# Experts' weights as the stationary operand in 24 up groups of a dense expert layer

## The reference, cut to what matters

```
q = h @ w_q; s1, s2 = scores of q's halves against two sets of 128 keys
e = ids of the 16 best pairs of each head;  w = softmax of their scores
act = gelu(u[e] . h) * w          # u: 16384 x 2048
y   = sum over heads and picks of act * vt[e]
x   = x + ga2 * y;  out = rmsnorm(x) * g_final
```

## Time and profile before

| | us |
|---|---|
| median of 3 runs | 3324.61 |
| lowest, highest | 3324.33, 3324.92 |
| the profiled execution | 3331.73 |
| its span, first to last instruction | 3330.1 |

### The profile page before, as it was taken

One profiled execution on the slowest core, in us unless ns is written; L12 is line 12 of the kernel. 1 busy time (PEld: TensorE's weight loads), 2 busy tenths in 40 slices (PEclk: granted clock), 3 DMA queues, 4 the chain that ended last, 5 costly groups with the idle time before them and its releaser, 6 DMA issues.

```text
span 3330.1 us, 41040 instructions
## 1 busy us (share of the span) xinstructions
PE 3311.5 (99%) x15198; PEld 2742.1 (82%) x15198; DVE 2232.1 (67%) x2112; ACT 1542.3 (46%) x1184; POOL 730.4 (22%) x559
## 2 busy tenths in 40 slices
PE   9999999999999999999999999999999999999999
PEld 8888888888787888878888888888888888888887
DVE  6674545688888788866677497444444777777777
ACT  7343334443333333353465346777776333333333
POOL 0000003400000000121000188888882000000000
PEclk9999999999999999999999999999999999999999
DMA  7555556888888888867555466777777666666663
GB/s 285 186 192 195 190 191 242 306 308 336 307 309 305 297 306 319 310 249 296 212 190 211 169 215 215 214 222 215 217 221 259 230 234 229 230 236 228 229 226 128
DMA packets 159557, 803.92 MB, mean 241 GB/s; under 512 B 51668, under 2 KB 52484, under 8 KB 70496
## 3 DMA queue, kind: packets, MB, share of 16 engines
q1 hardware_dynamic: 85728, 610.05, 50.3%
q0 software_dynamic: 67248, 170.03, 16.2%
q10 hardware_dynamic: 6480, 22.44, 1.8%
HBM read 759.23 MB, written 43.18 MB: 241 GB/s over the span
## 4 chain that ended last, share of the span: by engine, by line
PE 92%; DVE 3%; DMA 2%; issue 1%; ACT 1%; POOL 0%; SPq 0%; DVEq 0%; POOLq 0%; ACTq 0%
PE ps L2149 28%; PE ps L2151 28%; PE ps L2150 28%; PE ps L2189 2%; DVE adaacc L1532 2%; DMA adaraw<-in_w_ada 1%; PE ps L2226 1%; PE ps L2228 1%; PE ps L2227 1%; DMA raw<-in_w_first 1%; ACT hi L641 1%; PE ps L2337 0%; PE ps L2317 0%; DVE modrow L1543 0%; PE ps L2676 0%
## 5 line engine op out<-in xcount | busy, mean ns | idle before, releaser
L641 ACT CAST hi<-raw 128x2048 fp32r<-128x2048 f32 x571 | 1091.2, 1912 | 1617.9 <-PE ps L2151 1600.7
L1225 DVE TENSOR_TENSOR lo<-raw,hi 128x2048 fp32r<-128x2048 f32 x436 | 997.7, 2291 | 379.3 <-ACT hi L641 364.3
L2149 PE MATMUL ps<-hi,hT 128*128 128x512 f32 x2928 | 1152.4, 394 | 0.0
L2151 PE MATMUL ps<-hi,hT 128*128 128x512 f32 x2928 | 1140.4, 389 | 0.0
L2150 PE MATMUL ps<-lo,hT 128*128 128x512 f32 x2928 | 1139.9, 389 | 0.0
L2149 PEld LDWEIGHTS ps<-hi,hT 128*128 128x128 f32 x2928 | 549.9, 188 | 116.0 <-issue 4.8
L2151 PEld LDWEIGHTS ps<-hi,hT 128*128 128x128 f32 x2928 | 549.7, 188 | 115.6
L2150 PEld LDWEIGHTS ps<-lo,hT 128*128 128x128 f32 x2928 | 550.1, 188 | 111.0
L2011 DVE TENSOR_TENSOR lo<-raw,ps 128x2048 fp32r<-128x2048 f32 x96 | 219.7, 2288 | 297.6 <-ACT ps L1118 297.6
L581 POOL DMA_INDIRECT w_scratch<-picks,cell x256 | 396.7, 1550 | 80.1 <-issue 78.7
L2149 PE MATMUL ps<-hi,pactTh 128*128 128x512 f32 x992 | 388.7, 392 | 0.0
(11 more groups left out here) (415 smaller groups left out, 2668.9 us busy)
## 6 DMA issues: line engine op xcount, KB each, us to landing
raw<-in_w_peer SPq DMA_DIRECT2D x256, 1024.0 KB
raw<-in_w_ffn SPq DMA_DIRECT2D x132, 1024.0 KB
adaraw<-in_w_ada POOLq DMA_DIRECT2D x96, 1024.0 KB, 7.0
raw<-in_w_first SPq DMA_DIRECT2D x86, 1024.0 KB
raw<-in_w_second SPq DMA_DIRECT2D x72, 1024.0 KB
raw<-in_w_merge SPq DMA_DIRECT2D x28, 1024.0 KB
w_scratch<-zeros POOLq DMA_DIRECT2D x16, 1024.0 KB, 13.2
wc<-w_scratch POOLq DMA_DIRECT2D x32, 512.0 KB, 5.1
```

What stands on the lines that cost most here:

```text
L641: nc.scalar.copy(hi[:, s, :], raw[:, s, :]).then_inc(hi_done, 1)
L1225: V.tensor_tensor(lo[:, s, :], raw[:, s, :], hi[:, s, :].bitcast(F32), ALU.subtract).then_inc(lo_done, 1)
L2149: T.matmul(out, th[stat], hi[:, s, cut], start=start, stop=False)
L2151: return T.matmul(out, tl[stat], hi[:, s, cut], start=False, stop=stop)
```

## The change

In the up groups from number 8 (EARLY_TOP) on, 24 of 32, the operands change places. `expert_piece` takes 128 x 128 of the weights as stationary operand; the moving one is `hT[:, :, kt, :]`, both parts of the activations side by side (512 columns), for `hi`, and `hTh` alone (256 columns) for `lo`. That is 16 matmuls of 512 and 16 of 256 a piece. A tile of 128 experts stands in one bank: columns 0-255 hold hi x hTh + lo x hTh, columns 256-511 hold hi x hTl. Four tiles fill banks 0 to 3. ACT copies each second half into `gacc` (`second_halves`), DVE adds the first half (`expert_tiles`), ACT applies gelu to `gacc` in SBUF, and the store follows. Experts are on partitions now, so the product needs no turn: `peer_hi` and `peer_lo` read `pact` in SBUF.

Groups 0 to 7 keep the old up product; their hidden values are turned ahead of the product with the weights (`hidden_turn`), out of `hid`, and DVE multiplies out of PSUM. The dense weights lie in DRAM by expert (`w_d` is [16384, 256]), so the places of the picks, the clearing and the loads of `wc` change. One semaphore is merged into another on POOL.

Core of the diff:

```diff
# PE
+            def expert_piece(q, s, free):
+                pe.wait_ge(lo_done, 4 * q + (s + 1))
+                for e in range(4):
+                    if s == 0:
+                        free(e)
+                    for k in range(4):
+                        kt = 4 * s + k
+                        cut = slice(512 * k + P * e, 512 * k + P * e + P)
+                        if s == 0:
+                            T.matmul(ps[:, e, :], hi[:, s, cut], hT[:, :, kt, :], start=k == 0, stop=False)
+                            ins = T.matmul(ps[:, e, 0:SEQ], lo[:, s, cut], hTh[:, kt], start=False, stop=False)
+                        else:
+                            T.matmul(ps[:, e, 0:SEQ], lo[:, s, cut], hTh[:, kt], start=False, stop=False)
+                            ins = T.matmul(ps[:, e, :], hi[:, s, cut], hT[:, :, kt, :], start=False, stop=s == 3 and k == 3)
+                    if s == 3 and e < 3:
+                        ins.then_inc(sem("u_tile"), 1)
+                ins.then_inc(piece_used, 1)
+            def taken_out(g):
+                return lambda e: pe.wait_ge(sem("u_out"), 4 * g + (e + 1 - 4 * (EARLY_TOP + 1)))
+            expert_group(EARLY_TOP, lambda e: pe.wait_ge(sem("gelu"), EARLY_TOP - 1 + e // 2))
+            expert_group(EARLY_TOP + 1, taken_out(EARLY_TOP + 1))
+            def hidden_turn(g, u, m):
+                pe.wait_ge(sem(f"hid_in{u}"), 16 * m + 16)
+                if not isinstance(g, int) or g > 0:
+                    pe.wait_ge(sem("peer_product"), g)
+                turn(4, lambda k, m: hid[:, u, m, P * k:P * k + P]).then_inc(sem("peer_tr"), 1)
+            def first_turns(s):
+                if s == 1:
+                    pe.wait_ge(lo_done, 4 * (Q_PEER + EARLY))
+                if s in (1, 2):
+                    hidden_turn(s - 1, s - 1, 0)
+            expert_group(EARLY - 1, taken_out(EARLY - 1), first_turns)
...
-                    if j == 0:
-                        pe.wait_ge(sem("gelu"), b + 1)
                     if j < 4:
-                        wide_piece(q, s, 0)
+                        expert_piece(q, s, lambda e: pe.wait_ge(sem("y_sum"), 4 * b + 2))
# ACT
+            def second_halves(g, used):
+                for e in range(4):
+                    if e < 3:
+                        act.wait_ge(sem("u_tile"), 3 * g + (e + 1 - 3 * EARLY_TOP))
+                    else:
+                        act.wait_ge(piece_used, used)
+                    nc.scalar.copy(gaccT[:, SEQ * e:SEQ * e + SEQ], ps[:, e, SEQ:2 * SEQ]).then_inc(sem("pq_out"), 1)
             def early_group(g, u, copied=True):
                 for s in range(4):
+                    if s == 3 and not (isinstance(g, int) and g < EARLY_TOP):
+                        act.wait_ge(sem("hid_st"), 16 * g)
+                        second_halves(g, 4 * g + 4 * (Q_PEER + 1))
                     round_piece(g + (Q_PEER + 1), s)
...
-                gelu(g, u)
+                if isinstance(g, int) and g < EARLY_TOP:
+                    gelu(g, u)
+                    return
+                gelu_turned(g, 4 * g + 4 * (1 - EARLY_TOP))
+                store_turned(g)
             def peer_hi(b, u):
-                act.wait_ge(sem("peer_tr"), b + 1)
-                nc.scalar.copy(pactTh[:, u], quarters(4)).then_inc(sem("peer_hi"), 1)
+                act.wait_ge(sem("peer_product"), b + 1)
+                nc.scalar.copy(pactTh[:, u], pact[:]).then_inc(sem("peer_hi"), 1)
# DVE
+            def expert_tiles(g):
+                for e in range(4):
+                    dve.wait_ge(sem("pq_out"), 4 * g + (e + 5 - 4 * EARLY_TOP))
+                    tile = gaccT[:, SEQ * e:SEQ * e + SEQ]
+                    V.tensor_tensor(tile, ps[:, e, 0:SEQ], tile, ALU.add).then_inc(sem("u_out"), 1)
+            with dve.Fori(EARLY_TOP + 1, EARLY) as g:
+                for s in range(4):
+                    if s == 3:
+                        expert_tiles(g - 1)
+                    copied_rest(g, s)
# POOL
-                    part = w_d[16 * i:16 * i + 16].rearrange("t (a n) -> (t a) n", n=2048)
+                    part = w_d[1024 * i:1024 * i + 1024].rearrange("(r a) t -> r (a t)", a=8)
-            w_cells = w_d.rearrange("t (e o) -> (t e) o", o=1)
+            w_cells = w_d.rearrange("e (t o) -> (e t) o", o=1)
```

More of the change, by code:

```diff
@@ L144 @@
     "gy_T": "ACT: gelu of the turned gates", "qk_T": "DVE: turned queries and keys out of PSUM",
-    "wf_in": "DMA: forget weights", "wf_zero": "Pool: zeros around their two parts", "wfh": "ACT: their leading part", "wfl": "DVE: and rest; then identity and causal mask rounded", "f_mm": "PE: forget logits",
+    "wf_in": "DMA: forget weights", "wfh": "ACT: their leading part", "wfl": "DVE: and rest; then identity and causal mask rounded", "f_mm": "PE: forget logits",
     "lg_abs": "DVE: logits' size, then -|lambda|", "lg_exp": "ACT: their exponentials", "cum": "DVE: sums of log gates",
-    "sel_in": "Pool: zeros, then ones around the log gates' sums, then a row of zeros", "pair_in": "DMA: sums of four heads as rows", "scores2": "PE: heads' scores", "max2": "DVE: maxima",
+    "sel_in": "Pool: zeros around the forget weights, zeros, then ones around the log gates' sums, a row of zeros", "pair_in": "DMA: sums of four heads as rows", "scores2": "PE: heads' scores", "max2": "DVE: maxima",
     "exp2": "ACT: exponentials (two a head)", "turned2": "PE: turned probabilities", "probs2": "DVE: these out of PSUM",
@@ L158 @@
     "out2": "DVE: chunks out of PSUM", "out2_sum": "DVE: chunks added to x",
-    "pq_out": "ACT: query chunks out of PSUM", "pq_tr": "PE: turned", "pq_T": "DVE: turned chunks out of PSUM",
+    "pq_out": "ACT: query chunks, then second halves of tiles of experts, out of PSUM", "pq_tr": "PE: turned", "pq_T": "DVE: turned chunks out of PSUM",
     "keys_in": "DMA: both key sets", "key_scores": "PE: scores against them", "sc_out": "DVE: scores out of PSUM",
@@ L167 @@
     "hid_in1": "DMA: back, odd groups", "wc_in0": "DMA: weights of a group, slot 0", "wc_in1": "slot 1",
-    "peer_product": "DVE: hidden values times weights", "peer_tr": "PE: turned", "peer_hi": "ACT: leading part",
+    "u_tile": "PE: a group's first three tiles of experts", "u_out": "DVE: tiles of experts added from both halves",
+    "peer_product": "DVE: hidden values times weights", "peer_tr": "PE: first groups' hidden values turned", "peer_hi": "ACT: leading part",
     "peer_lo": "DVE: rest", "y_sum": "DVE: chunks out of PSUM, from two", "tail_in": "DMA: second gate", "gain_in": "DMA: last gains",
@@ L1147, in _ @@
                     peer_hi(0, 0)
-            gelu(EARLY - 1, 0, out=False)
+            gelu_turned(EARLY - 1, 4 * (EARLY - EARLY_TOP))
             def down_group(b, u, turn=True):
@@ L2098, in _ @@
                     dve.wait_ge(sem("peer_hi"), b + 2)
[L2099 removed]
+                    V.tensor_tensor(hTl[:, 0:4], pact[:], hTh[:, 0:4].bitcast(F32), ALU.subtract)\
                         .then_inc(sem("peer_lo"), 1)
```

150 lines of the change are left out of this document (85 added, 65 removed).

## The result

The changed kernel takes 3349.99 us in the median of 4 runs (3346.6 to 3351.48), the kernel before 3324.57 us beside it: a ratio of 1.0076, with a 95% interval of 1.0063 to 1.0088. The change costs 25.4 us; the forecast was 22.6. The profiled run took 3351.48 us with a span of 3349.9.

What follows compares the result with a forecast made beforehand. PE was taken to set the pace, at full clock. Turns -22.1, matmuls +9.7, borders +31.0, entry +2.3 and group 31 +1.7 sum to +22.6 us, on 3324.6 giving 3347.2 (own range 3333 to 3362, whole range 3328 to 3364).

Steps and rivals of the forecast that it cites:

- Borders: Starts of groups 9 to 30: PE waits 1.41 us for DVE to free a bank, 22 times, +31.0 us.
- the chain: Before each such start: ACT's rounding, DVE's rest 3.89 us later, its next operation 2.20 later; PE resumes at 6.95, not 5.54.
- tiles in time: Rival at group starts: DVE reaches the additions before PE finishes, so no 31.0 us; 3316 us, chance 9%.
- Turns: Down groups: 24 of 32 turns of hidden values go, 0.92 us of PE each, -22.1 us.
- Matmuls: Turned up groups: 16 matmuls of 512 and 16 of 256 a piece, 0.40 us more a group, +9.7 us.
- the operand in two parts: Up pieces: moving operand lying in hTh and hTl costs 0, bounds 0 and 15 us.
- Single places: Three single PE waits: group 8's third tile 2.3 us, group 31 1.7 us, group 30 0 (bound 1).
- Entry: Group 8's third tile: PE waits for gelu 7, 2.3 us.
- group 31: Group 31: PE waits for DVE to add the last chunk of group 29, 1.7 us.
- Weight loads: Rival in up pieces: loads make 256-wide steps 188 ns, 105 us more, 3452 us, chance 4%.
- picks: Scatter into the new weight layout: 0 us; rival: slower scatter, at 25% more about 3385 us, chance 5%.
- Clock: PE's granted clock: 1.4 us gaps shouldn't lower it, as it stayed 1.00 when PE stood 2.31 us.

Runs made afterwards that it cites:

- experiment 1: Changed kernel, with the first two of each turned group's four tiles copied and added before DVE's rest of the next group's third piece: 3328.62 us, ratio 1.0009.
- experiment 2: Changed kernel, with DVE forming the rests of groups 9 to 30 from SBUF, without ACT's copy in PSUM: 3441.08 us, ratio 1.0351.
- experiment 10: On experiment 4, the narrow product made 512 wide (lo also meets hTl), so all matmuls of a turned group are 512 wide: 3480.16 us, one run.
- experiment 11: On experiment 4, each 512-wide matmul made as two of 256, so all matmuls of a turned group are 256 wide: 3334.75 us, one run.
- experiment 6: On experiment 4, the 512-wide moving operand taken as one contiguous run (leading parts of two neighbouring input tiles; values differ): 3322.4 us, ratio 0.9996.
- experiment 12: On experiment 4, same-width matmuls in fours, in the two middle pieces in sixteens over all tiles, and other banks for the last pieces: 3316.51 us, ratio 0.9976.
- experiment 9: On experiment 4, every piece takes the 512-wide matmul first, then the 256-wide; before, later pieces had it the other way round: 3322.34 us, ratio 0.9993.
- experiment 4: On experiment 1, gelu 7 ahead of the last rounding, and group 31 waiting for group 29's last chunk only at its third tile: 3323.9 us, ratio 1.0000.
- experiment 7: On experiment 4 with same-width matmuls in fours, POOL instead of DVE adds gated sums to x before the last two down groups: 3319.76 us, ratio 0.9988.
- experiment 3: Changed kernel with EARLY_TOP 20 in place of 8, so twelve turned groups instead of twenty-four: 3340.15 us, ratio 1.0047.

## Why the prediction was right

The time, 3349.99 against 3347.2, and the sign came out by the mechanism that the forecast named. Point by point:

- **Borders.** Right in number (22), place, releaser and nearly in size: 1.32 us against 1.41. The two steps in the middle of the chain were exact (3.88 and 2.21); the rest was 0.1 shorter. Experiments 1 and 2 remove the chain in two different ways, and the gaps go in both. The rival "tiles in time" is thereby a description of another kernel, not of this one: experiment 1 is that rival, and it gives 3328.6 and not 3316.
- **Turns.** Right: 0.91 against 0.92 us each. Nothing came late in their place.
- **Matmuls.** The term that was mis-sized: 13 us against 9.7 here, and 20.4 us (24 x 0.85) once the borders are gone. The widths of 226.7 and 119.6 ns were each right, as experiments 10 and 11 show, but the forecast took them from stretches of one width each and added them. Its upper bound was laid on the wrong thing, the operand in two parts, which experiment 6 clears. In the changed kernel this error stayed small since in most groups only the first piece ran at 353 ns a pair and the others at 347. For the rival price of 3316 it would have mattered most.
- **Single places.** Entry 2.1 (2.3), group 31 1.6 (1.7). Two costs were missed. One is the clock behind the entry, below. The other: in the last piece PE waits 1.5 us for a bank. DVE comes to that chunk at 3320.95 where PE wants the bank at about 3320.8; it is late since the turned group's additions and the gated sums fall into the same stretch, where it idles nowhere for more than 0.16 us. The forecast did not follow DVE's queue beyond group 31. Experiment 12 gives the piece another bank, and the wait is gone.
- **Weight loads, picks.** Neither showed: 192 ns of loading stand behind steps of 120.0 ns over 24 groups (so the sentence of the Trainium skill, "TensorE: Matmul & The Clock Gate", What overlaps and what doesn't, that is weighed in the prediction doesn't hold for this kernel), and the picks took 1552 ns against 1548 before.
- **Clock.** Right for the 22 borders, behind none of which it fell. But the forecast had a pause of 2.3 us too, the entry, and judged only the 1.4 us ones. Behind the entry the granted clock fell from 2071.5 to 2074.9, and the matmuls took 1.5 us more. The row that the forecast leaned on, 2.31 us of waiting at a full clock, is one case; the trace of before has the other as well: PE waits 2.12 us until 1009.61, and the granted clock is at the lower level from 1010.7 to 1014.1. The page's digits do not show this, so "full in every slice" was not "full throughout".
- **Errors partly cancel:** borders -2.0, turns +0.3, matmuls +3.3, the last piece +1.5, entry and group 31 -0.3, the lower clock +1.5 make +4.3 in the trace; the median, 1.5 below the profiled run, shows +2.8. So a part of the closeness is luck; the sign and the size of the main terms are not.

**What stays open.** Why the alternating order has two paces. The same instructions in the same order run at 346.7 ns a pair in 62 of the 92 pieces of the changed kernel's groups 8 to 30, and near 353 in 29 of them and in 86 of experiment 1's 92. The difference lies in the steps behind the wide matmuls: 231 ns on average in the fast pieces, 236 in the slow ones, while the steps behind the narrow ones are 115 to 117 in both. The order in a pair (experiment 9) and the operand's layout (experiment 6) have been ruled out; blocks of one width lower the slow pace by a third. A pause of PE ahead of a group isn't what decides either: the changed kernel's groups 10 and 14 start behind a border like the others and stay at 353 through all four pieces. Most groups of the changed kernel switch from 353 to 347 with no interruption at all, where the first piece ends and the order in the pair turns round; in experiment 1 the same place switches nothing. But there, with no pause left ahead of it, group 30 has its last two pieces fast, right behind the turns between its pieces (fourteen pairs in 4.85 us, 346.4 ns):

```profile
2574.73 1.03 PE L2250 MATMUL ps<-ident,hid 128*128 128x128 f32 x8
...
2575.96 0.28 PE L2793 MATMUL ps<-hT,lo 128*128 128x256 f32 x1
...
2580.81 0.28 PE L2793 MATMUL ps<-hT,lo 128*128 128x256 f32 x1
```

Experiments 4, 6 and 9 show the same two fast pieces. So the pace is no property of the pair alone; what sets it was not tested.

## What to carry to other kernels

When a change makes one more engine pass a buffer before the bottleneck can have it back, write down the releasing engine's queue from the last moment at which the bottleneck holds it up, and compare with when the bottleneck returns: here that sum, from five rows of the kernel before, was within 0.1 us of the trace. The cure is seldom a faster engine but an earlier place in its queue; moving two small additions ahead of one long subtraction gave back 21 us. And a pace read in a stretch of equal instructions is a pace of that stretch: before instructions of two sizes are interleaved 1,536 times, a price for the mixture has to be kept in the range. Last, a pause can cost more than its length: read the granted clock in a narrow stretch behind it, since a slice of the page is too long to show it.

## What the runs showed of the hardware

- Matmuls of 512 and 256 columns in fp32r take 226.7 and 120.0 ns each by themselves, and up to 6.6 ns a pair more when they alternate (353.3, or 346.7 in some stretches of the same code); 350.8 in blocks of four, 349.1 with half of them in blocks of sixteen.
- Weight loads of 192 ns stay hidden behind steps of 120.0 ns, three loads in every 360 ns, over groups of 192 matmuls.
- One of POOL's indirect transfers that starts within DVE's subtraction with both inputs in SBUF takes 2.5 to 3.7 us in place of 1.55 (experiment 2), and ends 1.43 us behind it; a subtraction that starts within a transfer loses nothing. POOL's addition makes DVE's subtraction take 2.6 to 3.7 in place of 2.29 (experiment 7). With one input in PSUM (the changed kernel) the picks keep 1552 ns.
- While PE stood for 110 us in experiment 2 the granted clock of the stretch fell; after it, matmuls ran at the lower level of 1.2 GHz (0.43 us from a 512 wide one to the next, double of its columns' time at 2.4), and then at the upper one again. The changed kernel's 22 borders, with about 1.05 us of idle time each, had no such effect. Pauses near 2 us had it in some traces and not in others: behind 1.96 us it fell to 0.50 in the changed kernel and in experiments 2 and 3, and did not in experiment 1; before the change it fell behind 2.12 us and not behind 2.31. What decides was not tested. The stretches around experiment 2's long wait (length, busy times, granted clock, DMA share, GB/s) and PE's timeline after the wait:

```profile
2600.00:2700.00 100.00, 12.65 (x68) 11.32 (x69) 3.30 (x2) 3.49 (x4) 70.64 (x49) 0.54 0.28 32
2700.00:2800.00 100.00, 100.00 (x462) 83.15 (x461) 72.00 (x49) 39.35 (x26) 6.42 (x10) 1.00 0.63 233
```

```profile
2689.30 0.63 PE L2792 MATMUL ps<-hT,hi 128*128 128x512 f32 x1
2689.73 0.41 PE L2791 MATMUL ps<-hT,lo 128*128 128x256 f32 x1
```
